# Norms of the keys summed per head into 32 partitions, rooted once, and spread back by matmuls between r's tiles

## The reference

```python
r, k, v = einsum("nbtd,nde->nbte", h + xx * mu, w_rkv)
kk = heads(k * k_k)
kk = kk * rsqrt(maximum(sum(kk * kk, axis=-1, keepdims=True), 1e-24))
k  = k * (1 + (a - 1) * k_a)
y  = scan(r, decay, k, v, -kk, kk * a)      # over 256 tokens, in chunks of 64
```

## Time and profile before

| | us |
|---|---|
| median of three runs | 1961.63 |
| the profiled execution, its own time | 1961.79 |
| its span, first to last instruction | 1960.0 |
| TensorE matmuls, busy | 1915.0 |
| TensorE weight loads, busy (beside matmuls) | 1661.8 |
| VectorE, busy | 1434.8 |
| ScalarE, busy | 906.0 |
| GpSimd, busy | 121.9 |

### The profile page before, as it was taken

The page is one execution under the profiler, slowest core; times in us unless marked ns, Lnnn a source line. Parts: engine busy times, 40 slices in busy tenths (PEclk is TensorE's granted clock), DMA queues, the critical chain, the costliest instruction groups (busy, mean ns, idle before and its releaser), DMA issues.

```text
span 1960.0 us, 32673 instructions
## 1 busy us (share of the span) xinstructions
PE 1915.0 (98%) x12802; PEld 1661.8 (85%) x12802; DVE 1434.8 (73%) x2025; ACT 906.0 (46%) x1476; POOL 121.9 (6%) x126
## 2 busy tenths in 40 slices
PE   7999999998999989999999999999999999999998
PEld 5888888888888878888888888888888888888887
DVE  7997969324869988888877776444477967777876
ACT  3346321142335455555555555444455436645554
POOL 0000002000023200000000000000020000002200
PEclk9999999999999999999999999999999999999999
DMA  9996424554429746666555556555535544445553
GB/s 393 421 420 231 150 104 155 215 225 186 187 97 418 309 176 235 239 250 252 199 193 191 191 188 225 191 189 188 191 150 198 181 173 172 172 172 215 193 179 123
DMA packets 58936, 418.34 MB, mean 213 GB/s; under 512 B 6673, under 2 KB 7057, under 8 KB 12561
## 3 DMA queue, kind: packets, MB, share of 16 engines
q1 hardware_dynamic: 52210, 366.59, 50.9%
q0 software_dynamic: 6336, 46.14, 6.1%
q10 hardware_dynamic: 288, 4.19, 0.5%
HBM read 410.60 MB, written 6.29 MB: 213 GB/s over the span
## 4 chain that ended last, share of the span: by engine, by line
PE 87%; DVE 7%; DMA 3%; issue 2%; ACT 1%; POOL 1%; SPq 0%; DVEq 0%; ACTq 0%; POOLq 0%
PE ps L716 44%; PE ps L719 22%; PE ps L693 10%; PE ps L836 2%; DMA bk<-in_ada 2%; DVE ar L1921 1%; DMA zb<-in_ada 1%; PE ps L831 1%; PE ps L1107 1%; PE ps L852 1%; PE ps L1030 1%; POOL h L600 1%; DVE mixb L1973 0%; DVE bk L1728 0%; PE ps L923 0%
## 5 line engine op out<-in xcount | busy, mean ns | idle before, releaser
L716 PE MATMUL ps<-x_pair,whi 128*128 128x512 f32 x2464 | 790.3, 397 | 5.3 <-issue 2.8
L1750 DVE TENSOR_TENSOR wlo<-ring,whi 128x1024 fp32r<-128x1024 f32 x468 | 551.1, 1213 | 102.7 <-ACT whi L1269 98.8
L719 PEld LDWEIGHTS ps<-x_pair,wlo 128*128 128x128 f32 x2464 | 463.1, 188 | 95.4
L719 PE MATMUL ps<-x_pair,wlo 128*128 128x256 f32 x2464 | 510.7, 278 | 0.0
L1269 ACT ACTIVATE whi<-ring 128x1024 fp32r<-128x1024 f32 x468 | 462.5, 1031 | 97.4 <-PE ps L719 94.8
L716 PEld LDWEIGHTS ps<-x_pair,whi 128*128 128x128 f32 x2464 | 386.4, 188 | 23.2 <-issue 9.2
L1276 ACT ACTIVATE px<-ps 128x256 f32<-128x256 f32 x202 | 77.5, 384 | 443.0 <-PE ps L719 443.0
L716 PE MATMUL ps<-hid_pair,whi 128*128 128x512 f32 x688 | 216.8, 395 | 0.0
L719 PEld LDWEIGHTS ps<-hid_pair,wlo 128*128 128x128 f32 x688 | 129.3, 188 | 29.9
L693 PE MATMUL ps<-mixb,ring 128*128 128x256 f32 x640 | 142.2, 384 | 1.8 <-issue 1.8
L693 PEld LDWEIGHTS ps<-mixb,ring 128*128 128x128 f32 x640 | 122.6, 192 | 19.4 <-issue 2.2
(11 more groups left out here) (309 smaller groups left out, 2323.8 us busy)
## 6 DMA issues: line engine op xcount, KB each, us to landing
ring<-in_fi SPq DMA_DIRECT2D x86, 1024.0 KB, 4.8
ring<-in_zin SPq DMA_DIRECT2D x52, 1024.0 KB, 4.8
ring<-in_fo SPq DMA_DIRECT2D x32, 1024.0 KB, 4.9
ring<-in_ada SPq DMA_DIRECT2D x26, 1024.0 KB, 6.4
bk<-in_ada SPq DMA_DIRECT2D x22, 1024.0 KB, 18.0
ring<-in_wr SPq DMA_DIRECT2D x16, 1024.0 KB, 4.8
ring<-in_wv SPq DMA_DIRECT2D x16, 1024.0 KB, 4.8
ring<-in_wo SPq DMA_DIRECT2D x16, 1024.0 KB, 9.3
```

Of the source, the lines that this page charges most:

```text
L716: mm(ps[:, bank, 0:2 * S], whi[:, slot, j * P:(j + 1) * P], x2(k0 + j), start=first and j == 0, stop=False, skip_group_check=True)
L719: m = mm(ps[:, bank, 0:S], wlo[:, slot, j * P:(j + 1) * P], x2(k0 + j)[:, 0, :], start=False, stop=last and j == n - 1, skip_group_check=True)
L1750: V.tensor_tensor(wlo[:, hf % WB, 0:m], ring[:, u % RING, 1024 * x:1024 * x + m], whi[:, hf % WB, 0:m].bitcast(F32), ALU.subtract).then_in ...
```

## The change

The sums are taken with `sel`, a new constant of 128 x 62 whose window for tile i puts the sums of its two heads on rows 2i and 2i+1 of one bank; 16 matmuls accumulate, and the sums of all heads stand on 32 partitions x 256. ScalarE takes one root of that, VectorE one maximum and one reciprocal. `key_spread` multiplies it by columns of the identity, broadcast to 64, so that each head's row comes out on its 64 partitions: 16 matmuls behind r's tile 0 and 16 behind r's tile 2. VectorE's products read these from PSUM. The grams stand behind r's fifth tile (tile 4) instead of the eighth, and what followed tile 8 and 9 follows 5 and 6. ScalarE's powers of quarters 2 and 3 follow r's tiles 1 and 2. An unused buffer `sums` goes; later waits on the same semaphores count accordingly.

```diff
+    sel[np.arange(P), NH - 2 + np.arange(P) // HD] = 1.0
...
-            for q in range(8):
-                pe.wait_ge(k_sq, 2 * q + 2)
-                if q >= 4:
-                    pe.wait_ge(hs_root, q - 3)
-                for e in range(2):
-                    m = mm(ps[:, 4 + q % 4, e * S:(e + 1) * S], const("blk"), ar_i[:, 2 * q + e, 1, :], start=True, stop=True)
-                m.then_inc(hs_sum, 1)
+            for i in range(NT):
+                pe.wait_ge(k_sq, i + 1)
+                o = NH - 2 - 2 * i
+                m = mm(ps[0:NH, 4, 0:S], const("sel")[:, o:o + NH], ar_i[:, i, 1, :], start=i == 0, stop=i == NT - 1)
+            m.then_inc(hs_sum, 1)
+
+            def key_spread(half):
+
+                pe.wait_ge(hs_rec, 1)
+                for i in range(8 * half, 8 * half + 8):
+                    if half and i % 2 == 0:
+                        pe.wait_ge(hs_used, i // 2 - 3)
+                    for e in range(2):
+                        m = mm(ps[HD * e:HD * e + HD, 4 + i // 2 % 4, i % 2 * S:(i % 2 + 1) * S],
+                               ident[0:NH, 2 * i + e:2 * i + e + 1].to_broadcast([NH, HD]), sq_sum[0:NH, :],
+                               start=True, stop=True)
+                    if i % 2:
+                        m.then_inc(key_bc, 1)
 
             pe.wait_ge(mix_b, 5 * NT)
-            for k in range(8):
+            project("r", mixa, 0)
+            key_spread(0)
+            project("r", mixa, 1)
+            project("r", mixa, 2)
+            key_spread(1)
+            for k in range(3, R_AHEAD):
                 project("r", mixa, k)
...
-            project("r", mixa, 8)
+            project("r", mixa, R_AHEAD)
...
-                    project("r", mixa, 9)
+                    project("r", mixa, R_AHEAD + 1)
...
-            for k in range(10, NT):
+            for k in range(R_AHEAD + 2, NT):
...
-            for q in range(8):
-                act.wait_ge(hs_sum, q + 1)
-                A(ar_i[:, 2 * q:2 * q + 2, 1, :], ps[:, 4 + q % 4, :].rearrange("p (i s) -> p i s", s=S), ACT.Sqrt
-                  ).then_inc(hs_root, 1)
+            act.wait_ge(hs_sum, 1)
+            A(sq_sum[0:NH, :], ps[0:NH, 4, 0:S], ACT.Sqrt).then_inc(hs_root, 1)
...
-            for q in range(4):
-                for k in range(2 * q, 2 * q + 2):
-                    r_tile(k)
-                if q < 2:
-                    powers(q + 2)
-            act.wait_ge(tile_free, TILE["r"] + 8)
+            for k in range(R_AHEAD):
+                r_tile(k)
+                if k in (1, 2):
+                    powers(k + 1)
+            act.wait_ge(tile_free, TILE["r"] + R_AHEAD)
...
+            dve.wait_ge(hs_root, 1)
+            own(V.tensor_scalar(sq_sum[0:NH, :], sq_sum[0:NH, :], 1e-12, None, ALU.max))
+            V.reciprocal(sq_sum[0:NH, :], sq_sum[0:NH, :]).then_inc(hs_rec, 1)
             for b in range(8):
 
-                dve.wait_ge(hs_root, b + 1)
-                root, d = (ar_i[:, 2 * b:2 * b + 2, a, :] for a in (1, 0))
-                own(V.tensor_scalar(root, root, 1e-12, None, ALU.max))
-                own(V.reciprocal(root, root))
-                V.tensor_tensor(d, d, root, ALU.mult).then_inc(hs_used, 1)
+                dve.wait_ge(key_bc, b + 1)
+                d = ar_i[:, 2 * b:2 * b + 2, 0, :]
+                V.tensor_tensor(d, d, ps[:, 4 + b % 4, :].rearrange("p (i s) -> p i s", s=S), ALU.mult).then_inc(hs_used, 1)
```

More of the change, by code:

```diff
@@ L93 @@
               ("b_gate", NT), ("n_ple", NT)]
-CONST_COLS = [("ones", 1), ("eps", 2), ("ident", P), ("gmask", P), ("smask", S), ("blk2", 2), ("blk", P), ("cen", P),
+CONST_COLS = [("ones", 1), ("eps", 2), ("ident", P), ("gmask", P), ("smask", S), ("sel", 2 * NH - 2), ("blk2", 2), ("blk", P), ("cen", P),
               ("cos", S), ("sin", S), ("perm", P), ("amask", 3 * P)]
@@ L123, in constants @@
     put("blk", (i // HD == j // HD).astype(np.float32))
+    sel = np.zeros((P, 2 * NH - 2), np.float32)
+    sel[np.arange(P), NH - 2 + np.arange(P) // HD] = 1.0
+    put("sel", sel)
     put("blk2", (i // HD == np.arange(2)[None, :]).astype(np.float32))
@@ L199, in build @@
         res_gate = sb("res_gate", [P, 2 * NT])
-        sums = sb("sums", [P, 12])
         oka = sb("oka", [P, NT])
@@ L295, in build @@
         hs_used = sem("hs_used")
+        key_bc = sem("key_bc")
         pw_rdy = sem("pw_rdy")
@@ L420, in build @@
         GRAM_BANK = (0, 1, 4, 5, 2, 3, 6, 7)
+        R_AHEAD = 5
         Y_CUTS = (0, 4, 8, 12, 14, 16)
@@ L590, in wo_square @@
                     nc.gpsimd.tensor_copy(sq_sum[:], mixb[:, 0, :]).then_inc(sq_acc, 1)
-            pool.wait_ge(hs_sum, 9)
+            pool.wait_ge(hs_sum, 2)
             for j in range(NT):
@@ L1060, in _ @@
             gate_tile(1)
-            pe.wait_ge(hs_root, 9)
-            pe.wait_ge(hs_rec, 1)
+            pe.wait_ge(hs_root, 2)
+            pe.wait_ge(hs_rec, 2)
             for q in range(8):
@@ L1401, in powers, with r_tile @@
                 A(pend[:, 4 * q:4 * q + 4, :].rearrange("p i c -> p (i c)"), pxq[:, :, CH], ACT.Copy)
[L1403 to L1409, removed]
+            def r_tile(k):
+                act.wait_ge(pe_step, STEP["r"] + k + 1)
+                A(ar_tile(k, 1), split64(bank(TILE["r"] + k)), ACT.Copy).then_inc(tile_free, 1)
             powers(0)
             powers(1)
-            for q in range(4):
-                for k in range(2 * q, 2 * q + 2):
-                    r_tile(k)
-                if q < 2:
-                    powers(q + 2)
-            act.wait_ge(tile_free, TILE["r"] + 8)
+            for k in range(R_AHEAD):
[3 more added lines that the diff above has]
+            act.wait_ge(tile_free, TILE["r"] + R_AHEAD)
             for g in range(8):
@@ L1423, in _ @@
             mix("v")
-            with act.Fori(2, 4) as it:
-                for k in range(4):
-                    r_tile(k, it)
+            for k in range(R_AHEAD, NT):
+                r_tile(k)
             for q in range(4):
@@ L1476, in _ @@
                 A(ar[:, :, c, 0, :], y_new, ACT.Copy).then_inc(e_y, 1)
-            act.wait_ge(hs_sum, 9)
+            act.wait_ge(hs_sum, 2)
             A(rt[:], ps[:, 2, 0:64], ACT.Sqrt, scale=1.0 / HD, bias=const("eps")[:, 1:2]).then_inc(hs_root, 1)
@@ L2030, in _ @@
             v_bonus(1)
-            dve.wait_ge(hs_root, 9)
+            dve.wait_ge(hs_root, 2)
             V.reciprocal(rs[:], rt[:]).then_inc(hs_rec, 1)
```

## The result

The changed kernel is slower: 1972.4 us against 1962.23, medians of nine runs each (1968.41 to 1978.35 and 1959.37 to 1967.69), ratio 1.0047 [1.0035, 1.0059], some 9 us by the ratio. The forecast was 1965.7 with a range up to 1970.0. The direction was right, the size less than half. The profiled execution took 1972.4 us, 10.6 more than that of before.

What follows compares the result with a forecast made beforehand. TensorE, busy 1915.0 of 1960.0 us, was taken as the bound. Spread +7.6, wait -3.2, grams -0.3 make +4.1 on 1961.79, so 1965.9, and 1965.7 as median (0.16 lower); range 1961.0 to 1970.0.

Steps and rivals of the forecast that it cites:

- The sums cost nothing more: Norms' sums ahead of r: still 16 matmuls of 256 moving columns, now into 32 output rows, 7.07 us as before.
- One root, table load ahead: Before r's tiles: root from about 190.7, reciprocal ends at 193.1, asked for at 197.45, so covered by 4.3 us.
- The spread's price: 32 matmuls behind r's tiles: 16 pairs at 0.45, 7.2 us, plus 0.4 for shape changes; 7.6 us (6.8 to 8.8).
- No wait at the grams, 2.0 us to spare: At the first grams: scaled keys done at 230.7, TensorE there at 232.7, so the 3.2 us wait goes.
- The grams in 9.5 us at full clock: Grams behind r's fifth tile: masks set the pace, they end 0.3 us sooner, 9.5 instead of 9.8 us.
- The sum over this part, +4.1 us: Over r's first eight tiles and the grams: +7.6 - 3.2 - 0.3 = +4.1 us (+3.3 to +5.3).
- The third rival: Gaps between grams, or the spread on a quarter of the rows, bring a slow clock: +7.5, 1969.1; chance 0.15.
- no wait in the earlier trace hangs on these, so nothing is won: ScalarE's and VectorE's work on v and the triangular solve comes some 17 us sooner, winning nothing.
- The fourth rival: TensorE's shift against the loads removes v's first stall: -0.4, 1961.2; the second too: -2.2, 1959.4; chance 0.14.

Runs made afterwards that it cites:

- `R_AHEAD = 8`: Changed kernel with its grams put back behind r's eighth tile, where they were before: ratio 1.0041 [1.0028, 1.0055].

## Why the prediction was wrong

Point by point, against its own steps:

- *The sums cost nothing more*: 7.09 us against 7.07. Right.
- *One root, table load ahead*: the root ran at 191.04, the reciprocal took 1.74 us on 32 partitions and ended at 193.5; asked for at 198.03. Right, covered by 4.5 us (4.3 forecast).
- *The spread's price*: 201.63 - 198.03 = 3.60 us a half, 7.2 in all, so 0.45 a pair; r's tiles beside it took some 0.4 us more (233.25 - 190.93, less 7.2 and five tiles of 6.91, leaves 0.57, where the eight tiles before left 0.14). That makes 7.6 in all; 7.6 forecast. Right; the halves overlap, and the weight loads are hidden, though all use the same row group: those of one half were busy for 3.21 of its 3.60 us. The Trainium skill's sentence that a load overlaps a running matmul only where the row group differs ("TensorE: Matmul & The Clock Gate", Part 3) would have made it about 10.6, an estimate from 7.2 us and the prediction's 3.4 for the loads; the trace disagrees with it.
- *No wait at the grams, 2.0 us to spare*: VectorE's last scaled key began at 230.15 and took 1.22, TensorE came at 233.25. Right, 1.9 us.
- *The grams in 9.5 us at full clock*: 242.80 - 233.25 = 9.55. Right; the two gaps between them were 0.67 us rather than 0.85, and no slow stretch followed them.
- *The sum over this part, +4.1 us*: +4.2. Right, in this execution.
- *The third rival, the clock falls behind the spread*: not in the changed kernel's own trace (1.00 from 201.6 to 215.6 and from 219.2 to 233.2), but in three of the five other traces with the spread a stretch of 3.4 us at 0.50 follows one of its halves, at about 1.7 us and not the 3.4 that the rival was priced at. So it was in part luck that this sum came out: those three executions lost some 5.9 us up to the tile behind the grams.
- *"no wait in the earlier trace rows hangs on these, so nothing is won"*, of the moved work: right, by `R_AHEAD = 8`.
- *The fourth rival, the stalls among v's tiles*: this step failed. The prediction named the right place but priced only their going, 4.5 us and 1.8 us to be won, wrote that "Nothing in the profile says that the new place is better than the old", and put no price on a worse one: its sum holds this term at nothing. It put the cause down to the shift in time against the loads; the runs show a shift of code by half a block of instructions. The two stalls grew from 2.9 to 4.7 us, the second got a slow stretch of its own (446.10 to 452.93 at 0.50), and v's part lost 4.2 us.

So the mechanism that was forecast gives the first part of the loss, 4.2 of the pair's 10.6 us, to a tenth of a microsecond, and the sum lacked a second term as large as itself: 64 extra matmul records and as many weight loads in code that runs once. A shift of code made the kernel before 3 us slower and the changed one 4 us faster; that the term can come with either sign is what the range should have held. The slow stretches at 719 and 1453 us, some 3 us more in this pair, were in no step of the prediction, and their cause is open.

## What to carry to other kernels

Where TensorE sets the time, moving work from an idle engine onto it pays only for a wait that it removes: here 7.2 us were paid for 3.5, and placing one more tile ahead of the wait won the 3.5 for nothing. Where TensorE stalls on "issue" in straight-line code of small matmuls, ask for a packet of the instruction queue in or just ahead of the stall. If there is one, an edit in front can move the stall and change its length either way; before an edit of a few microseconds is judged, run it at several shifts of the code.

## What the runs showed of the hardware that was not expected

- A boundary between two 16 KB blocks of instructions, in 64x32 matmuls or up to 11 records behind them, cost TensorE 1.05 to 4.2 us where it stalled, at the same record to within two in kernels with the same code length in front, and 3.4 us with the DMA share at 0.27. Every such stall ended 1.2 to 1.6 us after the end of a packet of the instruction queue.
- The slow clock behind a gap does not follow from the gap alone: the stall of 2.8 us at the start of the second block's first projection is followed by a clock of 1.00 in the kernel before and of 0.51 in the changed one (1453.00 to 1456.40), with the same work ahead of it. With the same 2.8 us, nine of the twelve traces have the slow stretch there and three have not.
- The clock fell to 0.50 for 3.4 us behind a half of the spread, in which the timeline shows TensorE no idle time, in three of the six traces with it.
- Two halves of the partitions written in turn from the same 32 input rows ran beside each other: 0.45 us a pair of 256-column fp32 matmuls, against 0.43 for one.
